# A two-block model on one core: squares of x on one engine, weight splits a block earlier, the bias lines on another queue, and two merge gates inside the banded attention

## The reference, cut to what matters

```python
merged = (jax.nn.sigmoid(gate_a) * (y_a @ w_br_a[l])
          + jax.nn.sigmoid(gate_b) * (y_b @ w_br_b[l])
          + jax.nn.sigmoid(gate_c) * (y_c @ w_br_c[l]))
x = x + merged @ w_out[l]
```

## Time and profile before

| | |
|---|---|
| median of 3 runs | 3962.54 us |
| lowest, highest | 3956.91, 3962.54 us |
| the profiled execution's own time | 3960.44 us |
| its span | 3958.6 us |
| granted TensorE clock, mean | 0.959 |
| instructions | 60620 |

### The profile page before, as it was taken

The page is one execution under the profiler, slowest core; times in us unless marked ns, Lnnn a source line. Parts: engine busy times, 40 slices in busy tenths (PEclk is TensorE's granted clock), DMA queues, the critical chain, the costliest instruction groups (busy, mean ns, idle before and its releaser), DMA issues.

```text
span 3958.6 us, 60620 instructions
## 1 busy us (share of the span) xinstructions
PE 3691.1 (93%) x25506; PEld 3021.2 (76%) x25506; DVE 1956.9 (49%) x3020; ACT 1513.3 (38%) x2536; POOL 839.1 (21%) x832
## 2 busy tenths in 40 slices
PE   6989888999999989997999999998899799999998
PEld 3678877987888757786888788875677688878886
DVE  6656555535534565645333543437466533454343
ACT  4533223323323346644233422234565422343222
POOL 2222122221211123442110020202254311002120
PEclk7989998989999999998999999999999899999999
DMA  6310120013222202110223222220111022322222
GB/s 236 121 40 3 23 60 8 3 54 106 96 96 96 72 20 75 59 65 33 96 98 122 73 96 96 96 86 32 59 65 60 27 96 96 107 96 93 99 96 85
DMA packets 81111, 300.87 MB, mean 76 GB/s; under 512 B 8776, under 2 KB 9928, under 8 KB 79944
## 3 DMA queue, kind: packets, MB, share of 16 engines
q1 hardware_dynamic: 80840, 296.99, 22.0%
HBM read 292.76 MB, written 4.19 MB: 75 GB/s over the span
## 4 chain that ended last, share of the span: by engine, by line
PE 74%; DVE 11%; ACT 6%; issue 5%; POOL 3%; DMA 1%; SPq 0%; DVEq 0%; POOLq 0%; ACTq 0%
PE ps L208 72%; DVE wlo L239 2%; PE ps L213 1%; DVE he L247 1%; DMA wraw<-weights 1%; DVE ac L247 1%; ACT whi L227 1%; DVE hc L2419 1%; ACT ha L227 1%; DVE ha L239 1%; POOL p L243 1%; DVE ss L247 1%; ACT wp L228 1%; ACT L227 1%; DVE q L239 1%
## 5 line engine op out<-in xcount | busy, mean ns | idle before, releaser
L239 DVE TENSOR_TENSOR wlo<-wraw,whi 128x1024 fp32r<-128x1024 f32 x537 | 690.0, 1289 | 796.0 <-ACT whi L227 795.5
L208 PE MATMUL ps<-hh,whi 128*128 128x512 f32 x1840 | 728.7, 396 | 9.6 <-DVE hl L239 4.6
L208 PE MATMUL ps<-hl,whi 128*128 128x512 f32 x1840 | 720.5, 392 | 0.0
L208 PE MATMUL ps<-hh,wlo 128*128 128x512 f32 x1840 | 720.3, 391 | 0.0
L227 ACT ACTIVATE whi<-wraw 128x1024 fp32r<-128x1024 f32 x537 | 559.9, 1049 | 237.8 <-PE ps L208 187.1
L208 PEld LDWEIGHTS ps<-hh,whi 128*128 128x128 f32 x1840 | 347.8, 189 | 88.9 <-ACT hh L227 5.9
L208 PEld LDWEIGHTS ps<-hh,wlo 128*128 128x128 f32 x1840 | 348.0, 189 | 73.7
L208 PEld LDWEIGHTS ps<-hl,whi 128*128 128x128 f32 x1840 | 348.2, 189 | 70.5
L208 PE MATMUL ps<-u,u 64*64 64x64 f32 (+2 forms) x6016 | 229.2, 229 | 25.5 <-DVE u L239 16.8
L208 PEld LDWEIGHTS ps<-u,u 64*64 64x64 f32 (+1 forms) x6016 | 209.7, 140 | 42.8 <-DVE u L239 18.6
L208 PE MATMUL ps<-gh,whi 128*128 128x512 f32 x528 | 205.4, 389 | 0.0
(11 more groups left out here) (399 smaller groups left out, 7056.2 us busy)
## 6 DMA issues: line engine op xcount, KB each, us to landing
wraw<-weights SPq DMA_DIRECT2D x537, 512.0 KB, 3.2
x<-xT SPq DMA_DIRECT2D x2, 2048.0 KB, 9.8
bias_lines<-ln SPq DMA_DIRECT2D x1, 2048.0 KB
xmf<-memT SPq DMA_DIRECT2D x2, 1024.0 KB, 4.6
out<-x SPq DMA_DIRECT2D x1, 2048.0 KB, 6.2
bias<-bias_lines SPq DMA_DIRECT2D x1, 1536.0 KB, 8.7
con<-consts SPq DMA_DIRECT2D x1, 1379.0 KB, 16.6
ctxt<-ctxT SPq DMA_DIRECT2D x1, 1024.0 KB, 18.5
```

The costliest lines, as they stand in the source:

```text
L208: self.last, self.open = self.e.matmul(out, lhsT, rhs, start=start, stop=stop, skip_group_check=skip), True
L239: return self.e.tensor_tensor(out, a, b, op)
```

## The change

1. **Squares.** All 8 tiles of `x` and of the context are squared by ScalarE. GpSimd adds them in 4 pairs instead of to one tile, and `pe_sums` runs over 4 tiles: 16 products instead of 4 for `x`, 8 instead of 2 for the context. `pool_root` waits for the constants in both cases.
2. **Feeds.** In `dve_start` the calls that stood ahead of a wait with `ahead=1` now have `ahead=0` (they make what TensorE needs before it, and nothing of the next group), and `act_start` does the same for group 1. In `dve_chunks` the feed ahead of `dve_mod` makes two blocks of low parts instead of one, where a modulation row follows.
3. **Bias lines.** SP no longer issues the copy to `K.line`; ScalarE does, at the end of step 0 of projection (1, q, 1).
4. **Recurrence.** At `i == 0` the logarithms stand ahead of the values.
5. **Gates.** The gate projections b and c of j = 0 leave `pe_merge`. Gate b runs ahead of the scores of c = 1, ScalarE copies it out of PSUM to `L.stash` between the two exponentials of c = 0, later to `L.pre`, and the merge takes the sigmoid from there. Gate c runs ahead of the transposes of c = 4 in a bank that is held until the merge has read it. Each engine gets the feeds for them: ScalarE at c = 1 and 3, VectorE at c = 2 and 3.

```diff
+    def act_all_squares(self, tag, sq, xs, *ready):
+        act = self.act
+        for k in ks8:
+            act.wait_ge(*ready)
+            act.a(sq[k], xs[k], ACT.Square).then_inc(act("sq", *tag, k), 1)
+    def pool_pairs(self, tag, sq):
+        pool = self.pool
+        for k in range(0, 8, 2):
+            pool.wait_ge(self.act.at("sq", *tag, k + 1))
+            pool.tt(sq[k], sq[k], sq[k + 1], ALU.add).then_inc(pool("sq2", *tag, k // 2), 1)
...
-        K.pe_sums(lat, [K.HSQ[:, 0, :]], 4, lambda k: K.pool.at("acc", *lat))
+        K.pe_sums(lat, [K.HSQ[:, k, :] for k in range(0, 8, 2)], 4, lambda k: K.pool.at("sq2", *lat, k))
...
-        K.pe_sums(ctx, [K.CSQ[:, 0, :]], 2, lambda k: K.pool.at("acc", *ctx))
+        K.pe_sums(ctx, [K.CSQ[:, k, :] for k in range(0, 8, 2)], 2, lambda k: K.pool.at("sq2", *ctx, k))
...
-        K.act_feed("mod", 1, ahead=2)
+        K.act_feed("mod", 1, ahead=0)
...
-        K.dve_feed("mod", 2)
-        K.dve_squares(lat, [K.HSQ[:, k, :] for k in ks8], [K.x[:, k, :] for k in ks8], K.loaded("x"))
         K.dve_feed("mod", 2, ahead=2)
-        K.dve_squares(ctx, [K.CSQ[:, k, :] for k in ks8], [K.CT[:, k, :] for k in ks8], K.loaded("ctx"))
-        K.dve_feed("mod", 3, ahead=1)
+        K.dve_feed("mod", 3, ahead=0)
         K.dve_mod(2)
         K.dve_feed("mod", 3, ahead=2)
         K.dve_root(lat, 4, 1.0 / 1024)
-        K.dve_feed("mod", 0, ahead=1)
+        K.dve_feed("mod", 0, ahead=0)
...
-        K.dve_feed("mod", 1, ahead=1)
+        K.dve_feed("mod", 1, ahead=0)
...
+            if (hg, kind, i, step) == (1, "q", 1, 0):
+                act.wait_ge(act.at("ln"))
+                act.e.dma_start(K.line, K.LN.unsqueeze(1).broadcast_to([8, 128, 512])).then_inc(K.s_load["lines"], 16)
...
-                K.dve_feed("c", *z)
                 new, old = K.mod_step(hg, c)
+                K.dve_feed("c", *z, ahead=1 if new is None else 2)
...
                 gates(i, 1)
+                for dd in range(2):
+                    lns(i, dd)
                 if i == 0:
                     values()
-                for dd in range(2):
-                    lns(i, dd)
...
         for c in range(5):
+            if c == 1:
+                K.pe_gate(l, 0, "b")
...
+            if c == 4:
+                K.pe_gate(l, 0, "c", hold=True)
...
+            if c == 1:
+                K.act_feed("mg", l, 0, "b")
+            if c == 4:
+                act.wait_ge(act.at("stash", l), act.at("exped", l))
+                act.cp(L.pre, L.stash).then_inc(act("pre", l), 1)
+            if c == 3:
+                K.act_feed("mg", l, 0, "b", ahead=2)
...
+                if (c, e) == (0, 1):
+                    act.wait_ge(pe.at("mg", l, 0, "b"), K.ended("hgrn", l))
+                    act.cp(L.stash, ps["mg", l, 0, "b"]).then_inc(act("stash", l), 1)
+                    act.also("ps", "mg", l, 0, "b")
...
+            if c == 2:
+                K.dve_feed("mg", l, 0, "b")
+            if c == 3:
+                K.dve_feed("mg", l, 0, "b", ahead=2)
...
+    def pe_gate(self, l, j, n, hold=False):
+        K = self
+        K.proj(("mg", l, j, n), K.win(l, "g" + n, j), [(K.ps.take(K.pe, "mg", l, j, n, hold=hold), K.h["mix", l])])
...
-                K.proj(("mg", l, j, n), K.win(l, "g" + n, j), [(bg, h)])
+                if j > 0 or n == "a":
+                    K.pe_gate(l, j, n)
...
-            if b == K.block_of["c", 1, "q", 1] + NRAW:
-                K.load("lines", K.line, K.LN.unsqueeze(1).broadcast_to([8, 128, 512]), act.at("ln"))
```

More of the change, by code:

```diff
@@ L601, in layout @@
             L.wT = self.ring(f"wt{l}", [self.sb("wt", M + 9216 + 1536 * i, [128, 4, 384]) for i in range(2)], after_b)
+            L.stash = self.sb("pre", W + 19968, [128, 512])
+            L.pre = self.sb("pre", W + 33280, [128, 512])
             after_c = lambda l=l: K.ended("window", l)
@@ L912, in act_start @@
         K.act_feed("mod", 2)
-        K.act_squares(lat, [K.HSQ[:, k, :] for k in ks8], [K.x[:, k, :] for k in ks8], K.loaded("x"))
+        K.act_all_squares(lat, [K.HSQ[:, k, :] for k in ks8], [K.x[:, k, :] for k in ks8], K.loaded("x"))
         K.act_mod(2, K.mrow)
-        K.act_squares(ctx, [K.CSQ[:, k, :] for k in ks8], [K.CT[:, k, :] for k in ks8], K.loaded("ctx"))
+        K.act_all_squares(ctx, [K.CSQ[:, k, :] for k in ks8], [K.CT[:, k, :] for k in ks8], K.loaded("ctx"))
         K.act_mod(3, K.mrow)
         K.act_mod(0, K.mrow)
-        K.act_feed("mod", 1, ahead=2)
+        K.act_feed("mod", 1, ahead=0)
         K.act_shift(lat, range(4), K.x, K.HHI, 0)
@@ L970, in dve_scale @@
         for k in ks8:
-            dve.wait_ge(K.pe.at("rb", *tag), dve.at("gain", which), K.squared(tag, k))
+            dve.wait_ge(K.pe.at("rb", *tag), dve.at("gain", which), K.act.at("sq", *tag, k))
             dve.stt(v[:, k, :], v[:, k, :], K.gain[:, which, k:k + 1], ALU.mult, b[:, 0:T], ALU.mult).then_inc(dve("nv", *tag, k), 1)
@@ L985, in pool_start @@
         for tag, sq, nt in ((("lat",), K.HSQ, 4), (("ctx",), K.CSQ, 2)):
-            for k in range(1, 8):
-                pool.wait_ge(K.squared(tag, k - 1), K.squared(tag, k), pool.at("acc0", *tag, k - 1) if k > 1 else None)
-                pool.tt(sq[:, 0, :], sq[:, 0, :], sq[:, k, :], ALU.add).then_inc(pool("acc0", *tag, k), 1)
-            pool.also("acc", *tag)
-            if tag == ("lat",):
-                pool.wait_ge(K.loaded("consts"))
+            K.pool_pairs(tag, [sq[:, k, :] for k in ks8])
+            pool.wait_ge(K.loaded("consts"))
             K.pool_root(tag, nt)
@@ L2678, in act_window @@
                 act.also(f"ws{l}", *z)
+                act.also("exped", l)
                 K.act_sink(z, 4, K.vec(f"sink{l}")[:, c + 4 * e:c + 4 * e + 1])
@@ L2787, in dve_out @@
                 K.dve_square(tag[0:2], j, K.acc, K.accs)
+    def pe_gate(self, l, j, n, hold=False):
+        K = self
+        K.proj(("mg", l, j, n), K.win(l, "g" + n, j), [(K.ps.take(K.pe, "mg", l, j, n, hold=hold), K.h["mix", l])])
     def pe_merge(self, l):
         K, pe, L, ps = self, self.pe, self.L[l], self.ps
-        h = K.h["mix", l]
         perm = np.concatenate([np.concatenate([c * 64 + np.arange(64), (4 + c) * 64 + np.arange(64)]) for c in range(4)])
@@ L2796, in pe_merge @@
             for n in "abc":
-                bg, bb = ps.take(pe, "mg", l, j, n), ps.take(pe, "mb", l, j, n)
-                K.proj(("mg", l, j, n), K.win(l, "g" + n, j), [(bg, h)])
+                if j > 0 or n == "a":
+                    K.pe_gate(l, j, n)
+                bb = ps.take(pe, "mb", l, j, n)
                 cols = slice(j * 128, j * 128 + 128)
@@ L2801, in pe_merge @@
                 K.proj(("mb", l, j, n), [(f"w_br_{n}_2", l, r, cols) for r in rows], [(bb, L.y[n])])
+            if j == 0:
+                ps.drop("mg", l, 0, "c")
         K.pe_out(("wout", l), "w_out_2", l, L.merged)
@@ L2817, in act_merge @@
                 g = L.mg.take(act, l, j, n)
-                act.wait_ge(K.pe.at("mg", l, j, n))
-                act.a(g, ps["mg", l, j, n], ACT.Sigmoid).then_inc(act("mg", l, j, n), 1)
-                act.also("ps", "mg", l, j, n)
+                early = j == 0 and n == "b"
+                act.wait_ge(act.at("pre", l) if early else K.pe.at("mg", l, j, n))
+                act.a(g, L.pre if early else ps["mg", l, j, n], ACT.Sigmoid).then_inc(act("mg", l, j, n), 1)
+                if not early:
+                    act.also("ps", "mg", l, j, n)
                 K.act_feed("mb", l, j, n)
```

## The result

The changed kernel takes 3925.33 us, median of 4 runs (3921.69 to 3932.25), against 3962.54 for the kernel before: 37.2 less. The ratio of the fast runs is 0.9911 (35 us less), 95% interval 0.9894 to 0.9928, which is 28 to 42 us. The forecast was 3935, so it took some 10 us too little. The profiled execution took 3921.69, with a span of 3919.9; before 3960.4 and 3958.6.

What follows compares the result with a forecast made beforehand. TensorE was taken to bound the kernel, busy 93% of the span. Terms of -7.8 (bias lines), -6.6 (recurrence), -10.2 (gates), -1.0 (chunk feeds) and 0 (start) sum to -25.6 from 3960.4, so 3935; range 3919 to 3950.

Steps and rivals of the forecast that it cites:

- the likeliest case: Whole kernel: the forecast itself, 3935 us, with a range of its own of 3926 to 3945; chance 0.62.
- rival 1: Start: the 18 more products stand on the path and their 7 us are not caught up, 3942; chance 0.12.
- rival 2: Bias lines: queues served in order of issue, weights land behind the copy, TensorE waits some 8 us again, 3943; chance 0.12.
- rival 4: Bias lines: ScalarE stands still while the copy is issued, deciding from a 26 us hold on; 3971; chance 0.04.
- rival 3: Attention: gates not hidden, gate c at half clock and gate b's bank delaying VectorE; +10 for both layers, 3945; chance 0.10.
- What is late next: Bias lines: after the 7.29 us wait goes, the running projection's norm chain moves up 6 to 7; gain 6.9 to 9.5.
- The cost of the issue: Bias lines: ScalarE issuing the copy holds up work behind it in its queue; 0.3 us on the path (0 to 0.8).
- The 15.1 us of the earlier trace: Bias lines: landing time of weight blocks issued right behind the copy on SP, median of four, two issued before it.
- the bank's 1.7: Attention, gate b: its bank frees only after ScalarE's copy, delaying the last scores of c = 1; +1.7 us (0.5 to 3).
- the net cost of gate c: Attention, ahead of the transposes of c = 4: 6.4 us of products, faster work behind; net +2.0 us (0.5 to 6).
- a block made ahead closes the second gap: Chunks: where VectorE waits for the turned row, a block made ahead closes TensorE's later 0.62 us gap; term -1.0.
- a 2.74 us gap: Start: TensorE's earlier wait for ScalarE, taken to absorb the delay; were it not available, the start's bound is +5 us.

Runs made afterwards that it cites:

- the second timing: The changed kernel again, unaltered, timed together with its three variants on the same chip: 3926.57 us (5 runs), ratio 0.9909 to the kernel before.
- late on SP: Kernel before with only the bias lines issued about 60 us later or more, still on SP's queue: 3953.53 us (10 runs), ratio 0.9976.
- one tile of squares: Kernel before with only the new start, but GpSimd adding all eight squares into one tile and TensorE summing that: 3967.06 us (10 runs), ratio 1.0008.

## Why the prediction was right, and where its sizes were off

Its direction and its range hold. The median lies 0.7 below the likeliest case's own range of 3926 to 3945; the second timing (3926.57) lies 0.6 inside. No rival came about as a whole. The start costs nothing in time (rival 1). The copy does not stall the weights again, although the first block beside it takes 20.2 us (rival 2), and ScalarE is held by the issue for 1.26 us, not 26 (rival 4). Of the gates the costly case did not happen (rival 3). That the range holds is in part luck, for its ends do not follow from the terms: half of each term's bounds gives 3929 to 3948 and not 3926 to 3945, the gates' and the start's bounds reach 3928 and not 3919, and all five together 3924. Two of the five terms came at or beyond their fast ends. The forecast summed to -25.6 and the medians say -37; by term:

- **Bias lines, -7.8 forecast, -10 to -13 measured** (-12.9 in the changed kernel, -9.7 alone, -12.9 late on SP; in time -10). The step that failed is "What is late next". It let the chain of the norm move by 6 to 7 us only and the 2.45 stay. But the late block had stood in ScalarE's queue ahead of the copy of the running projection: that `zb` pair starts at 510.04, and started at 522.23 in the trace of before, 12.2 later and not 6. So both idle rows went, 9.7 us, and with them the low stretches 521.5 to 528.3 and 535.1 to 538.5, in which TensorE worked for 7.9 us at half clock, worth another 4. The bound of -9.5 had counted one idle row. The cost of the issue, 0.3 forecast with a bound of 0.8, came at that bound: TensorE waits 0.8 longer at 499.55 than at 500.05 before (1.82 against 1.03), and some 3.4 more is lost where a low stretch falls into the full load behind it. The 15.1 us of the earlier trace rows was misread as what a block behind the copy takes; the late one took 33.4.
- **Recurrence, -6.6 forecast, -6.5 measured.** The step holds row by row.
- **Gates, -10.2 forecast, -14.9 measured.** The saving of 10.9 a layer and the bank's 1.7 are as said (1.67). VectorE's feeds shift the third set of transposes by 2.2 in layer 0 and 2.5 in layer 1, as said (2.1). The step that failed is the net cost of gate c: +2.0 forecast, -1.2 and 0.0 measured (third set of transposes to the merge 20.24 against 21.47, and 20.39 against 20.41). The gate was to delay the transposes by 3.2 us and to shorten what stands behind them by 1.2. It delayed them by 0.5 and 2.5, and what stands behind them shrank by 1.6 (8.20 to 6.56) and 2.5 (7.13 to 4.64). I had taken the gap for 3.22 long, the idle time in the row. The gap that VectorE sets runs from the start of the products with the values to the transposes, 7.43 us whatever the clock, and these products fill 2.3 to 4.3 of it by the clock. I counted full clock for the gate and half clock for what stands ahead of it. Where the clock stayed low ahead of the gate (layer 1), the gate ended 2.5 late, and the transposes behind it found everything ready and took 2.3 us instead of 4.8: the stretch came out as long either way. The -1.2 in layer 0 is the low clock at the end of that stretch in the trace of before (1835.6 to 1842.4).
- **Feeds in the chunks, -1.0 forecast, 0.0 measured.** The step "a block made ahead closes the second gap" fails. The block is made ahead (136.52, not 138.10), but the gap belongs to the next one. Its low part waits for ScalarE's rounding, and that for TensorE, in the rows of before too (VectorE at 142.33 had waited 0.48 for ScalarE, 1.4 us ahead of TensorE's product at 143.70).
- **The start, 0 forecast, 0 measured in time,** -2.4 or +3.1 us at the first projection in two executions of one program, of which the clock is the larger part. The 16 sums of `x`, 6.2 at the forecast's 0.39 each, took 4.0 at a rising clock and 6.6 at the low one. The forecast's arrival, 64.6, lies between 61.98 and 67.45, and its bounds of -2.5 and +5 were the right size. The upper one was right by luck: it stood for the loss of a 2.74 us gap (1.05 of it is left in both executions), and it was the clock that cost the 3.1.

The terms by place are -13, -6.5 and -15, so -34.5. The changed kernel's profile has -4 more outside all edits (-2.0 between 555 and 885, -2.2 between 1925 and 2798), all of it stretches of the clock. Its second profile ends at 3933.6, -25.0 against before, by chance the forecast. So a pair of profiles tells this kernel's time to some 10 us only; the size of an edit is read between two blocks close around it, and the sum from medians.

What the working lacked as a whole: its terms took the clock of one execution's rows as a property of the place, and so did most of their bounds.

## What to carry to other kernels

A late transfer costs more than the idle row that it ends: follow what else stands behind the waiting instruction in its own queue, and add the half clock behind the gap. Look at transfers one by one: a median over blocks ahead of and beside a large copy says nothing about either. Read a gap from the point where the other engine's chain starts to the point where it ends (here 7.43 us in every trace without the gate), not from the bracket, which grows and shrinks with the clock of the work ahead of it. When timing edits of a few us in a kernel whose granted clock wanders, match instructions between traces and compare only across the edit.

## What the runs showed of the hardware

- The same program's profiled executions differ by 13.8 us (3921.69 and 3935.47), with 286 and 323 us of low clock in all. Within each variant the times of single runs fall by 1.6 to 3.4 us for each 0.001 of mean granted clock. The two have the same instructions and part in the first 50 us, where the clock rises at 35.3 in one and at 48.9 in the other.
- Earlier work does not stay earlier: 5.0 us gained at 67 us (one tile of squares) were gone at 491, with the clock low from 457.4 to 471.0 in between, and taking VectorE's gate feeds off its path in the attention (forecast 2.1 us a layer) left 0.6 and 1.0.
- A DMA issue on ScalarE holds it 1.26 us (0.83 on SP), while the 2 MB copy takes some 42. On one queue, blocks issued behind the copy wait for it: 33.4, 26.9, 18.0 and 9.0 us, all landed 1.6 us or more after its last packet. With the copy on ScalarE's queue they take 20.2, 14.8, 17.5 and 8.4 us in the changed kernel, against 3.1 to 3.4 with no copy, and the first lands 16.7 us before its last packet. The Trainium skill (DMA: Bandwidth & Descriptors, Queues, rings and completion order) has each DMA engine take turns between the rings that have work for it, packet by packet. These rows agree with turns and not with order of issue.
- A copy issued where SP has nothing else to issue delayed no weight block, but TensorE stood 6.64 us on "issue" while it ran, and a transfer of instructions came 17.3 us after its predecessor, against 8.7 in the changed kernel.
